# Front of an encoder block: x also loaded transposed, the norm's root applied to the results, LRU tiles read scaled between two scans

## The chip, the cores and the metric

One core of one Trainium2 chip. The metric is the device time of one execution in microseconds; 1294.04 us is the median of three runs (1293.98 to 1294.94). TensorE (PE) multiplies into eight PSUM banks of 128 x 512 float32. VectorE (DVE), ScalarE (ACT) and GpSimd (POOL) do elementwise work; SyncE (SP) only issues transfers here. Each engine runs its own list of instructions in order and waits on semaphores.

## The reference, cut to what matters

The kernel computes one encoder block: 16 meta tokens are put ahead of 1024 tokens, a group of recurrent heads (RG-LRU) and an attention group (MLA) share one input projection, and a ConvGLU feed-forward follows. The change touches only the first stage:

```python
hn = rmsnorm(h, norm_mix_g)      # h / sqrt(mean(h*h) + eps) * g, per token
proj = hn @ w_in                 # 1024 -> 512 + 512 + 256 + 128 + 32
x_lru, g_lru, c_q, c_kv, k_pe = split(proj)
xc = dwconv(x_lru)               # 4 taps along the tokens
y_lru = rg_lru_bidir(xc) * gelu(g_lru)   # two scans, forward and backward
q = rmsnorm(c_q) @ w_uq;  kv = rmsnorm(c_kv) @ w_ukv
```

The root of the norm belongs to a token and the gain g to a column of h. So `proj` can be had either from the normalised tokens, or from the raw tokens times (g * w_in), with each token's column of the result multiplied by its 1/root afterwards. Where a second rmsnorm follows (c_q, c_kv) the token's factor cancels, but for eps.

## The kernel before, in words

All products of the front are made of three fp32r products: each float32 operand is split into a high part (a copy rounded to fp32r) and a low part (value minus high), and `split_products` (L100 to L102) issues high*high, high*low and low*high.

The normalised, transposed tokens are kept in `xn_h` and `xn_l` (128 partitions x 8 k-blocks x 1040 tokens). Before the change a tile of 128 tokens (token-major) goes through a chain over four engines: SP loads it into one of four `x_tm` buffers, ACT squares it with a running sum (L440), DVE makes the variance (L652), ACT takes the root (L445), DVE takes the reciprocal (L658) and scales the tile by root and gain (L663), PE transposes it in eight matmuls (L889), ACT copies the high part out of PSUM (L450) and DVE the low part (L669). There are nine such tiles (16 meta tokens, then eight of 128).

The input projection is cut into twelve weight tiles of 128 columns (`tiles`): x0 to x3 (LRU input), c0 to c2 (the latents), k (rope part of the key), g0 to g3 (gate). Each weight tile is loaded (`load_w`, three buffers, a load waits until PE has finished the tile three before it), its high part made by ACT (`high_w`, L428) and its low part by DVE (`low_w`, L642). A unit is one weight tile times one stretch of tokens, 24 matmuls into one PSUM bank: x0 and c0 go in four stretches of 272 or 256 tokens as the tokens arrive, alternating, with the remaining transposes between their halves; all later tiles go in three stretches of 348 or 346.

The order of PE is written out: x0 and c0 alternating, then `order`: x1, G0, x2, c1, G1, x3, c2, G2, k, g0, G3, g1, g2, g3. G0 to G3 are the gate products of the recurrence, 12 units of three matmuls. The banks go round, so a unit waits until the earlier unit in its bank has been read (`free_bank`). ACT reads x, k, g and G out of PSUM, and squares and copies c (L469, L470); DVE makes the low part of c (L685) and with it frees c's bank.

For each of the four LRU tiles f: the four-tap convolution on DVE (`conv`, L695, L697), its high part on ACT (L477), low part on DVE (L705), G products on PE, `gates` on ACT (L487), `decay` on ACT (L496 to L502, three table loads), `gate_in` (L710) and `recurrence` on DVE: for each direction two elementwise operations (L716, L718) and a scan (L720, L723), then a sum (L726). `gelu(f)` on ACT writes `gel`, `gate_out` on DVE multiplies (L731). DVE's and ACT's order is written out too: in both, conv(f+2) stands behind recurrence(f), and the high part of its result is made on ACT ahead of decay(f+1), whose end starts recurrence(f+1).

After g3 the queries, keys and values of nine token tiles are made, then attention, output projection and feed-forward; the change leaves their code as it is. GpSimd's work in the front is a polynomial on 128 x 8 values (`softplus`, L359 to L370) and later the rope tables.

## Time and profile before

| | us |
|---|---|
| median of three runs | 1294.04 |
| the profiled execution, its own time | 1295.26 |
| span of its trace | 1293.2 |
| TensorE busy in the span | 1272.9 |
| VectorE busy | 998.6 |
| ScalarE busy | 769.5 |
| GpSimd busy | 148.3 |

The trace is of one execution of its own. The span runs from the first to the last instruction; 2.06 us lie outside it. Times below are microseconds from the start of the span.

### The profile page before, as it was taken

To read this page: it belongs to the slowest core of one execution; us is meant where nothing else is said; L and a number is where in the kernel's file an instruction comes from. 1 tells how busy PE (TensorE), PEld (TensorE's weight loads), DVE (VectorE), ACT (ScalarE), POOL (GpSimd) and SP (SyncE) were. 2 spreads that over 40 slices of the span, in tenths; PEclk is the share of its full clock that TensorE was granted. 3 is DMA by queue.
4 is the path that set the end of the run, shared out by engine and by line. 5 is a ranking of instruction groups with operands and counts; after the bars stand their busy time and mean duration, and the time that the engine had idled before them with its cause. 6 is when DMAs were issued, how large, how long until landed. Compare 5 with 4: busy or idle time off the path is not lost.

```text
span 1293.2 us, 18580 instructions
## 1 busy us (share of the span) xinstructions
PE 1272.9 (98%) x6202; PEld 1022.0 (79%) x6202; DVE 998.6 (77%) x1507; ACT 769.5 (60%) x1154; POOL 148.3 (11%) x175
## 2 busy tenths in 40 slices
PE   7999999999999999999999999999999999999998
PEld 7999998866667666687678888888888888888886
DVE  6677569778888876676879887787878887887856
ACT  6487648577676875633445565646474565656470
POOL 3000036400000001322300001000010000000010
PEclk9999999999999999999999999999999999999999
DMA  6111200000000014200143746576574846575667
GB/s 222 34 54 41 74 1 1 1 2 9 9 10 9 10 48 165 91 9 23 62 136 87 175 109 159 126 169 134 146 170 94 191 97 170 110 170 133 164 140 250
DMA packets 40939, 123.02 MB, mean 95 GB/s; under 512 B 7378, under 2 KB 8082, under 8 KB 34484
## 3 DMA queue, kind: packets, MB, share of 16 engines
q0 software_dynamic: 7200, 52.43, 21.4%
q1 hardware_dynamic: 33684, 69.86, 15.5%
q8 instruction: 34, 0.56, 0.2%
q14 instruction: 21, 0.17, 0.0%
HBM read 62.34 MB, written 59.80 MB: 94 GB/s over the span
## 4 chain that ended last, share of the span: by engine, by line
PE 85%; DVE 7%; ACT 4%; issue 2%; DMA 1%; SPq 0%; POOL 0%; DVEq 0%; ACTq 0%
PE banks L2967 31%; PE banks L3039 15%; PE banks L100 7%; PE banks L102 7%; PE banks L101 7%; PE banks L1954 2%; PE banks L2060 2%; PE banks L2104 2%; PE banks L2107 2%; PE banks L2061 2%; PE banks L2105 2%; PE banks L2062 2%; ACT e_f L1567 1%; PE banks L1909 1%; PE banks L1933 1%
## 5 line engine op out<-in xcount | busy, mean ns | idle before, releaser
L2967 PE MATMUL banks<-x_hi,slot_h 128*128 128x512 f32 x616 | 242.9, 394 | 2.9 <-DVE slot_l L2653 1.4
L2967 PE MATMUL banks<-x_lo,slot_h 128*128 128x512 f32 x616 | 243.5, 395 | 0.0
L2967 PE MATMUL banks<-x_hi,slot_l 128*128 128x512 f32 x616 | 242.9, 394 | 0.0
L2435 ACT ACTIVATE slot_h<-up_raw 128x512 fp32r<-128x512 f32 x127 | 79.9, 630 | 174.5 <-PE banks L2967 170.2
L2967 PEld LDWEIGHTS banks<-x_hi,slot_h 128*128 128x128 f32 x616 | 115.6, 188 | 31.6 <-DVE slot_l L2653 2.2
L2967 PEld LDWEIGHTS banks<-x_lo,slot_h 128*128 128x128 f32 x616 | 115.6, 188 | 27.0
L2967 PEld LDWEIGHTS banks<-x_hi,slot_l 128*128 128x128 f32 x616 | 115.7, 188 | 26.9
L2513 ACT ACTIVATE staged<-banks 128x1024 f32<-128x1024 f32 x100 | 101.6, 1027 | 40.9 <-PE banks L3039 40.9
L3039 PE MATMUL banks<-dn_h,a_h 128*128 128x512 f32 x280 | 110.4, 394 | 0.0
L2418 POOL DMA_DIRECT2D down_sums<-staged x50 | 44.2, 885 | 571.0 <-ACT staged L2513 496.0
L3039 PE MATMUL banks<-dn_h,a_l 128*128 128x512 f32 x280 | 109.6, 391 | 0.0
L3039 PE MATMUL banks<-dn_l,a_h 128*128 128x512 f32 x280 | 109.5, 391 | 0.0
L1567 ACT ACTIVATE e_f<-banks 128x1024 f32<-128x1024 f32 (+1 forms) x72 | 73.6, 1023 | 53.1 <-PE banks L2062 49.5
L100 PE MATMUL banks<-xn_h,win_h 128*128 128x346 f32 (+5 forms) x304 | 96.5, 317 | 1.5 <-DVE xn_l L669 1.5
L1716 DVE TENSOR_REDUCE lam_t<-banks 128x1 f32<-128x512 f32 x128 | 86.7, 687 | 14.1 <-PE banks L1954 14.1
L102 PE MATMUL banks<-xn_h,win_l 128*128 128x346 f32 (+5 forms) x304 | 95.2, 313 | 0.0
L101 PE MATMUL banks<-xn_l,win_h 128*128 128x346 f32 (+5 forms) x304 | 95.1, 313 | 0.0
L2653 DVE TENSOR_TENSOR slot_l<-up_raw,slot_h 128x512 fp32r<-128x512 f32 x127 | 87.0, 685 | 4.9 <-ACT slot_h L2435 4.7
L1761 DVE TENSOR_TENSOR e_l<-e_f,e_h 128x512 fp32r<-128x512 f32 x128 | 86.9, 690 | 1.2 <-ACT e_h L1574 1.0
L2796 DVE SCALAR_TENSOR_TENSOR gate_conv<-gate,par,gate_conv 128x1024 f32<-128x1024 f32 x44 | 55.6, 1283 | 24.1 <-ACT gate_conv L2527 19.7
L1574 ACT ACTIVATE e_h<-banks 128x1024 fp32r<-128x1024 f32 x64 | 65.2, 1018 | 0.0
L2744 DVE TENSOR_TENSOR dn_l<-dn_raw,dn_h 128x512 fp32r<-128x512 f32 x70 | 48.0, 686 | 20.2 <-ACT dn_h L2499 20.2
(357 smaller groups left out, 2870.8 us busy)
## 6 DMA issues: line engine op xcount, KB each, us to landing
down_sums<-staged POOLq DMA_DIRECT2D x50, 1024.0 KB, 8.0
up_raw<-in_w_up SPq DMA_DIRECT2D x88, 256.0 KB, 3.7
dn_raw<-in_w_down SPq DMA_DIRECT2D x22, 512.0 KB, 6.7
win_raw<-in_w_in SPq DMA_DIRECT2D x11, 512.0 KB, 3.3
x_tm<-in_x_tm SPq DMA_DIRECT2D x8, 512.0 KB, 5.9
wo_raw<-in_w_out SPq DMA_DIRECT2D x16, 256.0 KB, 4.0
h<-in_x_tm SPq DMA_DIRECT2D x8, 512.0 KB, 5.7
down_sums<-h SPq DMA_DIRECT2D x3, 1024.0 KB, 6.6
```

What stands on the lines that cost most here:

```text
L100: nc.tensor.matmul(out, w_h, x_h, start=first, stop=False)
L101: nc.tensor.matmul(out, w_h, x_l, start=False, stop=False)
L102: return nc.tensor.matmul(out, w_l, x_h, start=False, stop=last)
L1567: nc.scalar.activation(e_f[g % 3][0:n], s_ps(g)[0:n], ACT.Exp, scale=SCALE)
L1574: ins = nc.scalar.activation(e_h[g % 3], s_ps(g), ACT.Exp, scale=SCALE)
L1716: ins = nc.vector.tensor_reduce(mx3[:, i:i + 1], side, AX.X, ALU.max)
L1761: nc.vector.tensor_tensor(e_l[(g - 1) % 2][:, cs], e_f[(g - 1) % 3][:, cs], f32(e_h[(g - 1) % 3][:, cs]), ALU.subtract).then_inc(sem["e_lo ...
L2435: nc.scalar.activation(s_h[slot], x, ACT.Copy).then_inc(sem["up_hi"], 1)
L2513: nc.scalar.activation(staged[b][:, 2 * p:2 * p + 2, :], bank(4 + 2 * p, 2).rearrange("p (i n) -> p i n", i=2), ACT.Copy).then_inc(sem["dn ...
L2653: nc.vector.tensor_tensor(s_l[slot], x, f32(s_h[slot]), ALU.subtract).then_inc(sem["up_lo"], 1)
L2967: ins = nc.tensor.matmul(o, s[slot][:, k], xs[w], start=fresh and k == 0 and n == 0, stop=k == 3 and n == 2, skip_group_check=not fresh)
L3039: ins = nc.tensor.matmul(bank(4 + i), x[:, ts], w, start=k in FRESH and n == 0, stop=n == 2, skip_group_check=k not in FRESH)
```

## The change

- The tokens are loaded twice: transposed and raw (`x_raw`, four stretches, the first in two halves), and token-major in pairs of tiles (`x_tm`) for the squares alone. The transposes, the scaling of tiles and the broadcast load of the gain go.
- ACT and DVE split the raw transposed tokens into high and low parts straight from SBUF.
- The gain is multiplied into each weight tile before it is split: by GpSimd (`gain_w`), for tile 1 by DVE.
- ACT squares the nine token tiles in a row; then one variance, one root, one reciprocal for all. DVE builds eight diagonal blocks of the roots, and PE multiplies them by a matrix of ones (`rows_of_r`, units R), which gives in every partition the row of all tokens' 1/root; ACT copies it to SBUF (`x_rb`).
- DVE reads the x and g tiles out of PSUM, multiplied by that row (`read_scaled`); x2 and x3 are read between the two scans of a recurrence. The gelu is one activation of 1040 columns from SBUF.
- The eps of the second norms is scaled by the token's variance (`v_kv_eps`, `v_q_eps`), and the rope part of the key is scaled when it is read.
- The banks: the eight first units have one bank each, then R, then the round starts at bank 7. PE's order of tiles stays.

```diff
+    raw_at = (M_LRU, M_YL, M_YL + 2 * P * KD, M_LRU + (META + 2 * P) * KD)
+    x_raw = [place(f"x_raw{c}", at, (KD, 2 * P + (0 if c else META))) for c, at in enumerate(raw_at)]
+    x_sb = [place(f"x_tm{b}", at, (2, D)) for b, at in
+            enumerate((M_C + T, M_C + 4 * T, M_CSQ + T, raw_at[3] + 2 * P * KD))]
+    x_rb, x_dg = place("x_rstd_rows", M_KPE + T, (T,)), place("x_diag", M_KPE + 2 * T, (XT, P))
+    x_var, x_r = stat[:, 0, 0:NT], stat[:, 0, 16:16 + NT]
+    x_std, v_kv_eps, v_q_eps = stat[:, 1, 0:NT], stat[:, 0, 48:48 + NT], stat[:, 1, 48:48 + NT]
+    mix_g = par[:, COLS["mix_g"]:COLS["mix_g"] + KD]
...
-    ST_BANK = (4 + shared) % 8
+    AT = 7
+    ST_BANK = (AT + shared) % 8
     rest = [u for u in later_units[shared:] if u[0] != "st"]
-    bank_no = [n % 4 for n in range(len(first_units))] + [(4 + n) % 8 for n in range(shared)] +\
+    bank_no = list(range(len(first_units))) + [1, 3, 5] + [(AT + n) % 8 for n in range(shared)] +\
               [ST_BANK if u[0] == "st" else (ST_BANK + 1 + rest.index(u) % 7) % 8 for u in later_units[shared:]]
+    act_reads = [u for u in units if u[0] in "RGk"]
+    dve_reads = [u for u in first_units if u[0] == "c"] + [u for u in first_units if u[0] == "x"] +\
+                [u for t in (("x", 1), ("x", 2), ("c", 1), ("x", 3), ("c", 2), ("g", 0), ("st", 0), ("g", 1), ("g", 2), ("g", 3))
+                 for u in units_of(*t)]
...
-        def load_x(j):
-
-            if j == 0:
-                sp.dma_start(x_meta[0:META], dram["meta_tm"]).then_inc(sem["x_meta_in"], 16)
-                return
-            if j > 4:
-                sp.wait_ge(sem["xn"], j - 3)
-            sp.dma_start(x_sb[(j - 1) % 4], dram["x_tm"][P * j - P:P * j, :]).then_inc(sem["xt_in"][(j - 1) % 4], 16)
+        def load_raw(c):
+
+            if c >= 2:
+                sp.wait_ge(sem["xr_in"][c - 2], 16)
+            arrived = sem["xt_in"][3] if c == 1 else sem["xr_in"][c - 2]
+            sp.dma_start(x_raw[c], dram["x_raw"][c - 1]).then_inc(arrived, 16)
+
+        def load_raw_0(w):
+            sp.dma_start(x_raw[0][:, HALVES[w]], dram["x_raw0"][w]).then_inc(sem["xr_in"][w], 16)
+
+        def load_tm(b):
...
+            if b == 3:
+                sp.wait_ge(sem["xt_in"][3], 16)
+            sp.dma_start(x_sb[b], dram["x_tm"][2 * P * b:2 * P * (b + 1), :].rearrange("(t p) d -> p t d", p=P))\
+              .then_inc(sem["xt_in"][b], 16)
...
         sp.dma_start(ident, dram["ident"]).then_inc(sem["ident_in"], 16)
-        load_x(0)
-        load_x(1)
-        sp.dma_start(mix_g, dram["mix_g"].unsqueeze(0).broadcast_to([P, D])).then_inc(sem["mix_g_in"], 16)
         load_w(0)
-        load_x(2)
+        load_raw_0(0)
         load_w(1)
-        load_x(3)
-        load_x(4)
+        load_raw_0(1)
+        load_raw(1)
+        load_raw(2)
+        load_raw(3)
+        load_tm(0)
+        sp.dma_start(x_meta, dram["meta_tm"]).then_inc(sem["x_meta_in"], 16)
+        load_tm(1)
+        load_tm(2)
+        load_w(2)
+        load_tm(3)
         load_gw(0)
-        load_w(2)
-        for j in range(5, NL):
-            load_x(j)
         for name in ("gqk", "rope_c", "rope_s"):
             sp.dma_start(con[name], dram[name]).then_inc(sem["con_in"], 16)
         load_w(3)
...
+        def gain_w(n):
+            cols = ROPE if tiles[n][0] == "k" else P
+            pool.wait_ge(sem["w_in"][n % 3], 16 * (n // 3 + 1))
+            w = w_raw[n % 3][:, :, 0:cols]
+            nc.gpsimd.tensor_tensor(w, w, mix_g.unsqueeze(2).broadcast_to((P, KD, cols)), ALU.mult).then_inc(sem["w_gain"], 1)
+
+        pool.wait_ge(sem["par_in"], 16)
+        gain_w(0)
         softplus()
+        pool.wait_ge(sem["w_gain"], 2)
+        for n in range(2, len(tiles)):
+            gain_w(n)
...
-            act.wait_ge(sem["w_in"][n % 3], 16 * (n // 3 + 1))
+            act.wait_ge(sem["w_gain"], n + 1)
...
-        def high_x(j):
-            n, t0 = LOADS[j]
-            act.wait_ge(sem["x_t"], j + 1)
-            nc.scalar.activation(xn_h[:, :, t0:t0 + n], tp(j)[:, :, 0:n], ACT.Copy).then_inc(sem["x_hi"], 1)
-            wait_unit(act, ("x", f, c))
-            nc.scalar.activation(xpad[:, 2 + c0:2 + c0 + cn], ps(("x", f, c))[:, 0:cn], ACT.Copy)\
-              .then_inc(sem["read_act"], 1)
...
+                act.wait_ge(sem["xt_in"][(j - 1) // 2], 32 if (j - 1) // 2 == 3 else 16)
+            x, i = x_of(j)[0:n], x_col(j)
+            nc.scalar.activation(x, x, ACT.Square, accum_out=x_var[0:n, i:i + 1]).then_inc(sem["x_sq"], 1)
+        def std_x():
+            act.wait_ge(sem["x_var"], 2)
+            for n, ts in PARTS:
+                nc.scalar.activation(x_std[0:n, ts], x_var[0:n, ts], ACT.Sqrt).then_inc(sem["x_std"], 1)
+        def high_x(c, w):
+            c0, cn = LOAD_CH[c]
+            act.wait_ge(sem["xt_in"][3] if c else sem["xr_in"][w], 16)
+            nc.scalar.activation(xn_h[:, HALVES[w], c0:c0 + cn], x_raw[c][:, HALVES[w]], ACT.Copy).then_inc(sem["x_hi"], 1)
+
+        def copy_r():
+            for c, (c0, cn) in enumerate(((META, 4 * P), (META + 4 * P, 4 * P), (0, META))):
+                wait_unit(act, ("R", 0, c))
+                nc.scalar.activation(x_rb[:, c0:c0 + cn], ps(("R", 0, c))[:, 0:cn], ACT.Copy).then_inc(sem["read_act"], 1)
...
-            if f:
-                act.wait_ge(sem["y_lru"], f)
-            for c, (c0, cn) in enumerate(CH):
-                wait_unit(act, ("g", f, c))
-                nc.scalar.activation(gel[:, c0:c0 + cn], ps(("g", f, c))[:, 0:cn], ACT.Gelu_apprx_tanh)\
-                  .then_inc(sem["read_act"], 1)
+            wait_read(act, ("g", f, 2))
+            nc.scalar.activation(gel, gel, ACT.Gelu_apprx_tanh).then_inc(sem["gelu"], 1)
...
+        act.wait_ge(sem["lam_e"], 1)
+        nc.scalar.activation(x_std[:, 0:1], con["lam_t"][:, 1, 0:1], ACT.Sqrt)
+
+        high_x(0, 0)
+        high_w(0)
+        high_x(0, 1)
+        high_w(1)
+        high_x(1, 0)
+        high_x(1, 1)
+        read_c(0, 0)
+        square_x(1)
+        square_x(2)
         square_x(0)
-        high_x(2)
-        std_x(3)
...
+        for j in range(5, NL):
+            square_x(j)
+        std_x()
+        read_c(0, 2)
+        high_w(2)
+        high_gw(0)
+        read_c(0, 3)
+        copy_r()
         high_xc(0)
         high_w(3)
-        for c in range(3):
-            read_x(1, c)
         high_w(4)
...
+        def gain_w(n):
+            dve.wait_ge(sem["w_gain"], n)
+            dve.wait_ge(sem["w_in"][n % 3], 16 * (n // 3 + 1))
+            nc.vector.tensor_tensor(w_raw[n % 3], w_raw[n % 3], mix_g.unsqueeze(2).broadcast_to((P, KD, P)), ALU.mult)\
+              .then_inc(sem["w_gain"], 1)
...
-        def scale_x(j):
-            nc.vector.scalar_tensor_tensor(out=xn[j % 2][0:n], in0=x_of(j), scalar=x_r[0:n, j:j + 1], in1=mix_g[0:n],
-                                           op0=ALU.mult, op1=ALU.mult).then_inc(sem["xn"], 1)
...
+        def high_low_x(c):
+            c0, cn = LOAD_CH[c]
+            dve.wait_ge(sem["xr_in"][c - 2], 32)
+            for w in range(2):
+                link(nc.vector.tensor_copy(xn_h[:, HALVES[w], c0:c0 + cn], x_raw[c][:, HALVES[w]]))
+                low_part(c, w)
+
+        def low_part(c, w):
+            c0, cn = LOAD_CH[c]
+            nc.vector.tensor_tensor(xn_l[:, HALVES[w], c0:c0 + cn], x_raw[c][:, HALVES[w]],
+                                    f32(xn_h[:, HALVES[w], c0:c0 + cn]), ALU.subtract).then_inc(sem["x_lo"], 1)
+
+        def low_x(c, w):
+            dve.wait_ge(sem["x_hi"], 2 * c + w + 1)
+            low_part(c, w)
+
+        def var_x():
+            dve.wait_ge(sem["x_sq"], NL)
+            for n, ts in PARTS:
+                nc.vector.tensor_scalar(x_var[0:n, ts], x_var[0:n, ts], 1.0 / D, EPS, ALU.mult, ALU.add)\
+                  .then_inc(sem["x_var"], 1)
+        def diag_x():
+            dve.wait_ge(sem["x_std"], 2)
+            for n, ts in PARTS:
+                link(nc.vector.reciprocal(x_r[0:n, ts], x_std[0:n, ts]))
+            dve.wait_ge(sem["ident_in"], 16)
+            nc.vector.tensor_tensor(x_dg, ident.unsqueeze(1).broadcast_to((P, XT, P)),
+                                    x_r[:, 0:XT].unsqueeze(2).broadcast_to((P, XT, P)), ALU.mult).then_inc(sem["x_dg"], 1)
+            nc.vector.tensor_scalar(x_dgm, ident[0:META, 0:META], x_r[0:META, XT:NT], None, ALU.mult)\
+              .then_inc(sem["x_dg"], 1)
+            dve.wait_ge(sem["x_var"], 2)
+            for n, ts in PARTS:
+                link(nc.vector.tensor_scalar(v_kv_eps[0:n, ts], x_var[0:n, ts], EPS, None, ALU.mult))
+                link(nc.vector.tensor_scalar(v_q_eps[0:n, ts], x_var[0:n, ts], EPS * EPS, None, ALU.mult))
+
+        def read_scaled(u, out):
+
+            c0, cn = chunk(u)
+            wait_unit(dve, u)
+            nc.vector.tensor_tensor(out, ps(u)[:, 0:cn], x_rb[:, c0:c0 + cn], ALU.mult).then_inc(sem["read_dve"], 1)
+
+        def read_x(f):
+            if f == 0:
+                dve.wait_ge(sem["set_up"], 3)
+                wait_read(dve, ("R", 0, 2))
+            else:
+                dve.wait_ge(sem["conv"], f)
+            for u in units_of("x", f):
+                c0, cn = chunk(u)
+                read_scaled(u, xpad[:, 2 + c0:2 + c0 + cn])
+
+        def read_g(f):
+            if f:
+                dve.wait_ge(sem["y_lru"], f)
+            for u in units_of("g", f):
+                c0, cn = chunk(u)
+                read_scaled(u, gel[:, c0:c0 + cn])
...
+                    if f + 2 < LF:
+                        read_x(f + 2)
...
-            wait_read(dve, ("g", f, 2))
+            dve.wait_ge(sem["gelu"], f + 1)
             nc.vector.tensor_tensor(yl[:, f, :], yl[:, f, :], gel, ALU.mult).then_inc(sem["y_lru"], 1)
...
-        scale_x(1)
+        low_x(0, 0)
         low_w(0)
+        gain_w(1)
+        low_x(0, 1)
         low_w(1)
+        low_x(1, 0)
+        low_x(1, 1)
+        high_low_x(2)
+        high_low_x(3)
+        low_c(0, 0)
+        low_c(0, 1)
+        var_x()
+        diag_x()
+        low_c(0, 2)
+        low_w(2)
+        low_gw(0)
+        low_c(0, 3)
+        read_x(0)
         conv(0)
         low_xc(0)
         low_w(3)
+        read_x(1)
         conv(1)
         low_w(4)
 
...
         low_w(9)
+        read_g(0)
+        low_w(10)
         gate_out(0)
-        low_w(10)
...
+        wait_tile(dve, ("st", 0))
+            nc.vector.tensor_tensor(kpe[0:n, ts], st_ps[0:n, ts, 16:16 + ROPE],
+                                    x_r[0:n, ts].unsqueeze(2).broadcast_to((n, m, ROPE)), ALU.mult).then_inc(sem["kpe_tm"], 1)
         nc.vector.tensor_tensor(uq_l, uq_raw, f32(uq_h), ALU.subtract).then_inc(sem["uq_lo"], 1)
-        gate_out(1)
+        read_g(1)
         dve.wait_ge(sem["ukv_hi"], 1)
         nc.vector.tensor_tensor(ukv_l, ukv_raw, f32(ukv_h), ALU.subtract).then_inc(sem["ukv_lo"], 1)
+        gate_out(1)
+        read_g(2)
         gate_out(2)
+        read_g(3)
         gate_out(3)
...
-            elif bank_no[n] >= 4:
-                pe.wait_ge(sem["x_lo"], NL)
-
-        def transpose_x(j):
-            n, _ = LOADS[j]
-            if j == 0:
...
-            for k in range(KD):
-                ins = nc.tensor.transpose(tp(j)[:, k, 0:n], xn[j % 2][0:n, P * k:P * k + P], ident[0:n, 0:n])
-            ins.then_inc(sem["x_t"], 1)
...
-                if (kind, f) == ("x", 0) and k == KD // 2 and 2 * c + 3 < NL:
-                    transpose_x(2 * c + 3)
+                if (kind, f) == ("x", 0) and k % (KD // 2) == 0:
+                    pe.wait_ge(sem["x_lo"], 2 * c + 1 + k // (KD // 2))
                 ins = split_products(nc, ps(u)[0:m, 0:cn], w_h[n % 3][:, k, 0:m], w_l[n % 3][:, k, 0:m],
                                      xn_h[:, k, c0:c0 + cn], xn_l[:, k, c0:c0 + cn], k == 0, k == KD - 1)
...
+        def rows_of_r():
+
+            for c in range(3):
+                free_bank(("R", 0, c))
+                pe.wait_ge(sem["x_dg"], 2 if c == 2 else 1)
+                if c == 2:
+                    ins = nc.tensor.matmul(ps(("R", 0, c))[:, 0:META], ones[0:META], x_dgm, start=True, stop=True)
+                else:
+                    for i in range(4):
+                        ins = nc.tensor.matmul(ps(("R", 0, c))[:, P * i:P * i + P], ones, x_dg[:, 4 * c + i],
+                                               start=True, stop=True)
+                ins.then_inc(sem["unit_done"], 1)
-            if n == 0:
-                pe.wait_ge(sem["ident_in"], 16)
-            for _ in range((10, 0, 4, 5)[n]):
-                nc.tensor.matmul(bank(3)[:, 0:P], ident, ident, start=True, stop=True)
-
-        for j in range(3):
-            warm(j)
-            transpose_x(j)
-        warm(3)
+            for _ in range(n):
+                nc.tensor.matmul(bank(7)[:, 0:P], ident, ident, start=True, stop=True)
+
+        pe.wait_ge(sem["ident_in"], 16)
+        warm(24)
         for c in range(len(LOAD_CH)):
-            pe.wait_ge(sem["x_lo"], 2 * c + 3)
             project(("x", 0, c))
-            if 2 * c + 4 < NL:
-                transpose_x(2 * c + 4)
             project(("c", 0, c))
+        pe.wait_ge(sem["set_up"], 3)
+        rows_of_r()
         for kind, f in order:
             if kind == "G":
                 gate_products(f)
```

## Rows read from the trace of the kernel before

**Rows 1.** The page, part 1: busy time and share of each engine.
```profile
PE 1272.9 (98%) x6202; PEld 1022.0 (79%) x6202; DVE 998.6 (77%) x1507; ACT 769.5 (60%) x1154; POOL 148.3 (11%) x175
```

**Rows 2.** Busy time by stretch: stretch, its length, each engine's busy time, PEclk, DMA.
```profile
0.00:18.60 18.60, 12.13 (x62) 11.57 (x62) 9.09 (x19) 12.63 (x22) 10.12 (x33) 1.00 0.83 307
18.60:48.30 29.70, 29.47 (x244) 29.05 (x245) 20.09 (x29) 16.96 (x35) 0.00 (x0) 1.00 0.22 68
```

**Rows 3.** PE's waits up to 235 us: who waited for whom, total, times, longest.
```profile
PE banks L100 <- DVE xn_l L669: 1.5, 2, 1.3
```

**Rows 4.** PE in order of time: start, duration, line, operands, idle time before.
```profile
3.77 4.64 PE L942 MATMUL banks<-ident 128*128 128x128 f32 x20 [3.77 <-DMA ident<-in_ident]
...
18.62 0.39 PE L100 MATMUL banks<-xn_h,win_h 128*128 128x272 f32 x1 [1.26 <-DVE xn_l L669]
...
28.22 1.03 PE L889 MATMUL banks<-ident,xn 128*128 128x128 f32 x8
29.01 0.36 PE L100 MATMUL banks<-xn_h,win_h 128*128 128x256 f32 x1
...
47.76 0.32 PE L100 MATMUL banks<-xn_h,win_h 128*128 128x348 f32 x1
...
59.21 0.32 PE L100 MATMUL banks<-xc_h,gw_h 128*128 128x348 f32 x1
...
116.38 0.32 PE L100 MATMUL banks<-xc_h,gw_h 128*128 128x348 f32 x1
```

**Rows 5.** Transfers of the first 20 us: GB/s in forty slices of 0.5 us.
```profile
GB/s 0 0 0 70 139 185 74 188 270 377 361 311 246 279 385 393 418 459 401 410 410 418 442 410 418 410 393 418 418 442 393 393 418 393 401 238 41 0 0 0
```

**Rows 6.** The page, part 6: transfers by line, KB, median us to landing.
```profile
win_raw<-in_w_in SPq DMA_DIRECT2D x11, 512.0 KB, 3.3
```

**Rows 7.** ACT in order of time, columns as in rows 4.
```profile
6.58 1.06 ACT L440 ACTIVATE x_sq<-x_tm 128x1024 f32<-128x1024 f32 x1
7.55 0.19 ACT L440 ACTIVATION_READ_ACCUMULATOR x_sq<-x_tm 128x1 f32 x1
...
9.36 1.06 ACT L428 ACTIVATE win_h<-win_raw 128x1024 fp32r<-128x1024 f32 x1 [1.20 <-DMA win_raw<-in_w_in]
...
88.35 0.55 ACT L470 ACTIVATE c_h<-banks,par 128x346 fp32r<-128x346 f32 x1
...
95.54 1.07 ACT L477 ACTIVATE xc_h<-xc 128x1040 fp32r<-128x1040 f32 x1 [0.40 <-DVE xc L697]
...
193.63 1.28 ACT L599 ACT_TABLE_LOAD   x1
...
196.66 0.69 ACT L623 ACTIVATE k_sq<-banks,lam_t 128x512 f32<-128x512 f32 x1 [0.58 <-PE banks L102]
```

**Rows 8.** DVE by group, 18 to 231 us: shapes, count, busy us, mean ns, idle before.
```profile
L697 DVE SCALAR_TENSOR_TENSOR xc<-xpad,par,xc 128x1040 f32<-128x1040 f32 x12 | 15.6, 1302 | 0.4
L642 DVE TENSOR_TENSOR win_l<-win_raw,win_h 128x1024 fp32r<-128x1024 f32 x10 | 12.5, 1248 | 5.3 <-ACT win_h L428 5.3
L720 DVE TENSOR_TENSOR_SCAN y_lru<-lru_a,lru_x 128x1040 f32<-128x1040 f32 x4 | 9.3, 2324 | 0.1
L695 DVE TENSOR_SCALAR xc<-xpad,par 128x1040 f32<-128x1040 f32 x4 | 3.3, 817 | 2.4 <-ACT xpad L460 2.4
L685 DVE SCALAR_TENSOR_TENSOR c_l<-banks,par,c_h 128x346 fp32r<-128x346 f32 x4 | 2.1, 570 | 0.0
```

**Rows 9.** DVE in order of time around recurrence(0) and recurrence(1).
```profile
77.24 1.24 DVE L716 SCALAR_TENSOR_TENSOR lru_w<-lru_a,lru_w 128x1040 f32<-128x1040 f32 x1 [1.88 <-ACT lru_a L502]
...
105.38 1.24 DVE L716 SCALAR_TENSOR_TENSOR lru_w<-lru_a,lru_w 128x1040 f32<-128x1040 f32 x1 [1.88 <-ACT lru_a L502]
...
116.55 1.54 DVE L685 SCALAR_TENSOR_TENSOR c_l<-banks,par,c_h 128x348 fp32r<-128x348 f32 x3
```

**Rows 10.** GpSimd in order of time, 543 to 548 us.
```profile
543.85 1.29 POOL L1399 TENSOR_TENSOR y_l<-y_lru,y_h 128x512 fp32r<-128x512 f32 x1
545.10 2.18 POOL L1399 TENSOR_TENSOR y_l<-y_mla,y_h 128x512 fp32r<-128x512 f32 x1
```

**Rows 11.** DVE in order of time, the same stretch.
```profile
544.11 2.10 DVE L1652 TENSOR_TENSOR y_sum<-y_sum,y_sq 128x1024 f32<-128x1024 f32 x1 [0.73 <-ACT y_sq L1496]
```

152 lines of the change are left out of this document (35 added, 117 removed).

## The prediction, made before the changed kernel ran

> **What bounds the kernel now.** I read the page first: PE is busy 98% of the span [rows 1]. Then the table by stretch: in the first 18.6 us PE is busy 12.1, mostly with warming products, and from 18.6 to 48.3 it is busy 29.47 of 29.70, at the full granted clock of 1.00, its 2.4 GHz level [rows 2]. PE's waits for the split tokens are 1.5 us in two, up to 235 us [rows 3]. So a microsecond taken from PE's work in the front, or from its start, is worth one as long as DVE and ACT keep up. PE's own order of time gives the marks [rows 4]: first projection 18.62, x1 from 47.76, G0 from 59.21 (called T1 below), G2 from 116.38, which is T1 + 57.2. A tile of three stretches (72 products) is 59.21 - 47.76 = 11.45, a set of G (36) half of it, 5.7.
>
> **The start.** The eight first units took 47.76 - 18.62 = 29.1. In between stand six transposes of eight products (29.01 - 28.22 = 0.79, with the slow restart about 0.9 [rows 4]: 5.4) and waits of 0.5; 23.2 stay. When can they begin after the change? The transfers: in rows 5 the sum up to 9.0 us is 2.08 MB, then 0.41 MB per us. Weight tile 0 was waited for until 9.36 [rows 7], when 2.2 MB had moved and 1.8 had been asked for up to it; so a transfer lands when some 0.4 MB more than the queue up to it has moved. The new queue, from the sizes in the diff: par, ident and w0 0.67 MB, landing 6.4; first half of stretch 0, 1.2 MB, 8.0; w1 9.2; second half 10.6; stretch 1 13.1; stretches 2 and 3 15.6 and 18.5; the token tiles two by two 21, 23.6, 26.1 and, behind w2, 29.7 (10.5 MB with what follows). GpSimd's product for w0 has 1024 columns; 512 took 1.29 [rows 10], so 2.5: 6.4 to 8.9. ACT: high x (1088 columns) 8.1 to 9.2, high w0 to 10.2 (1.06 [rows 7]). DVE: low x to 10.6, low w0 to 11.8 (1.25 [rows 8]). PE begins at 11.8 and waits 0.8 for its second half, since DVE has the gain of w1 before it (low w1 ends at 15.3, just as c0 wants it). After that DVE is ahead: two subtractions for stretch 1, then four copies and four subtractions for 2 and 3 (a copy isn't in the trace; I take 0.82 of a one-input operation [rows 8], ends 0.5 and 1.3, which change nothing) end at 25.9, four microseconds before they are due. c0's last unit ends at 11.8 + 0.8 + 23.2 = 35.8: 12.0 gained so far.
>
> **What is late next: the root, and the list behind it.** A square takes 1.15 with its sum [rows 7]; the last two wait for the last token tiles, 29.7, and end at 32.3; variance, root, reciprocals and the diagonal of 1024 columns on DVE (1.25) end at 34.8. R is eight products of 128 float32 columns, 0.23 each (4.64 for 20 [rows 4]): PE from 35.8 to 37.6. But x1 wants c0's last bank, which DVE frees at the end of a list behind the diagonal: meta diagonal and four small operations (1.0), low c (0.45, scaled from 0.57 for 346 columns [rows 8]), low w2 (1.2), low gate weights (0.7), low c: 38.5. All of it hangs on the last token tiles: a microsecond later there is one later here. And w3's gain meets it: its load goes out when x0 is done, 32.9, lands 3.3 later [rows 6], at 36.3.
>
> **The port between GpSimd and VectorE.** In rows 10 and 11 DVE's sum of 1024 columns starts at 544.11 and takes 2.10 in place of 1.25, while a GpSimd product runs until 545.14; then GpSimd's next takes 2.18 in place of 1.29. Each waits for the other's whole instruction, and the one that waits gets the next turn. From w2 on GpSimd has ten gains, 2.5 us each (the k tile 0.7). w3's takes the turn between low w2 and the low gate weights: 38.5 becomes 40.9. x1 starts at 40.9: **gained here 47.8 - 40.9 = 6.9** (ends: 9.3 without a meeting, 4.5 if w4's gain gets a turn too). T1 becomes 52.3; the four scaled reads of x0 (1.7), conv(0) (0.8 + 3 x 1.3 [rows 8]) and its split end at about 50, hidden under x1.
> The Trainium skill, "SBUF — State Buffer", section "Who interferes with whom", has the same lock for a VectorE instruction with two SBUF inputs, and frees one with a single SBUF input outside the two-port modes; by that the scaled reads out of PSUM escape and the scans and multiplies don't. If the gains never met DVE the whole sum would be 4.5 better; that is rival A.
>
> **The loop.** Times from the new T1. PE's period is 57.2 / 2 = 28.6. The round over DVE and ACT was 105.38 - 77.24 = 28.1 [rows 9]. The x tiles leave ACT: it follows G0 unit by unit, ends 6.2, high xc 7.3, and from there to the recurrence 8.8 (95.54 + 1.07 to 105.38 [rows 7, 9]): recurrence(0) at T1 + 16.1, before 18.0. But between its two scans stand three reads of 346 columns (0.57 by low c [rows 8], 1.6 in all), and the round becomes 29.8. Without the port: recurrence(1) from T1 + 46.0 to 58.4 (before 46.2 to 57.0), c2's first bank read at 59.3; G2's sixth unit wants it at 57.2 + 2.4 = 59.6. Before, it was read at T1 + 57.9 [rows 9]: 1.7 us of slack shrink to 0.3. With the port: w6 is asked for when x2 is done, 17.1, and its gain comes at 20.5, during the scan; it then holds up the multiply behind the reads by 0.8. w8's comes at 49.0, in recurrence(1): 0.8 if it waits for the scan, 2.5 if it goes before, I take 1.6. The read comes at 61.7 and **PE stops 2.1** (ends 0 and 6.9, the latter with full turns of w6, w8 and w9 in the two recurrences). In the third round gates(3) start 2 us before G3's eighth unit wants their first bank; w9 and w10 use that up and I count nothing. At its end read_g (1.6 each) and gate_out of g1 and g2 are through at T1 + 133.4, before g3 (133.9 + 2.1).
>
> **The tail.** Let T be the end of g3's last unit, 193.1 by the q products that follow at once. Before: table load at 193.63, k squares at 196.66 = T + 3.5 [rows 7]. After: DVE reads the unit (0.55) and q's first products wait, since it lies in their bank; gelu of 1040 columns 1.1, load 1.28, root; k squares at T + 4.1. **0.6 lost.** Everything behind is as before.
>
> Edits at nothing: the squares in a row (ACT is busy 17.0 of 29.7 [rows 2], and loses the reads of x), the early root on one column (loads the table at 3.1, before any token has landed), softplus behind the first gain (ends by 30, wanted at 53), the eps vectors (counted above). With the cover gone each costs its own 0.2 to 1.2.
>
> **Sum.** 6.9 - 2.1 - 0.6 = 4.2 saved. Against the profiled execution's own 1295.26 (1.2 above the median of the runs) that is 1291.1; against the median 1294.04 it is 1289.8, which I predict.
>
> **Rivals.**
> A. The port costs nothing on the path: w3 lands after the gate weights are split, w6 and w8 fall into gaps. 9.3 - 0.6 = 8.7: 1285.3. For it: DVE is idle a third of the stretch to 48.3 [rows 2]. Against: both marks lie where DVE works back to back. 0.20.
> B. The doubled load of x (4.2 MB more before w3) is the bound. At 307 GB/s, the mean of the first 18.6 us [rows 2], the last token tiles land at 34.5, and root, R and x1 are each late by 4.8: 4.2 - 4.8, so 1294.6, no change, with PE idle ahead of R. For it: twice the bytes. Against: 393 to 459 GB/s in the slices after 8 us [rows 5]; that mean is low by its ramp. 0.15. The skill's "SBUF — State Buffer", section "A bandwidth-pool intuition that's wrong (but worth ruling out)", gives HBM to one core about 358 GB/s; by that they would land 2.6 late and 1.6 be saved, 1292.4. The rows contradict it here.
> C. Slower: the port decides. If w3's and w4's gains both go before low c, x1 starts at 43.3 (4.5 gained); if w6, w8 and w9 each take a full 2.5 inside a recurrence, the read of c2 comes at T1 + 66.5 and PE stops 6.9: 4.5 - 6.9 - 0.6 = -3.0: 1297.0. It decides from 6.3 us of PE stops behind x1's start. For it: the one that waits gets the next turn [rows 10, 11]. Against: each gain must meet a busy stretch at its beginning. 0.12.
> D. The forecast: 0.53, its own range 1287.5 to 1292.
>
> **Range and chances.** 1285.2 to 1295.5 takes in A's price, B and the half of C next to it; the ends of the unknown costs (9.3 to 4.5 at x1, 0 to 6.9 in the loop) are reached only when they fall together. Faster by over 0.2% (2.6 us, about what a measurement of this kernel tells from no change): A, and D but for its upper end, 0.70. Within: B and that end, 0.18. Slower: C, 0.12.
>
> **What would show it.** First projection at 11.8 (after 14: the gain of w0 or the transfers). x1 at 40.9, PE idle before it, and DVE's low gate weights lasting about 3 us beside GpSimd's gain. The diagonal before R's turn; a wait of PE for it is B. A wait of PE inside G2 for low c, with lengthened multiplies beside gains. k squares 0.6 later behind g3 than before. I am wrong if G2 has no wait, or if PE's time from x1 to the k squares grows by over 5 us.

## The result: 0.19% slower, and the profile after

The changed kernel takes 1295.95 us (median of 20 runs, 1291.13 to 1301.74), the one before 1293.47 (20 runs on the same chip, 1291.81 to 1297.27). The ratio is 1.0019, 95% interval 1.0010 to 1.0028: 2.5 us slower where 4.2 less had been forecast. The time goes with the granted clock of TensorE, averaged over each run: the run at 0.999 took 1291.13, ten at 0.996 or 0.997 took 1293.1 to 1296.4, the one at 0.992 took 1301.74. The profiled execution has 1295.51 of its own (span 1293.3, mean clock 0.996).

The page, part 1, the same view as [rows 1]: PE is busy 3.1 us less in a span of the same length, POOL 26.6 us more.

```profile
PE 1269.8 (98%) x6158; PEld 1019.5 (79%) x6158; DVE 1010.2 (78%) x1521; ACT 760.5 (59%) x1123; POOL 174.9 (14%) x186
```

PE in order of time, the same view as [rows 4]. The row that stands by itself is of the kernel before: the start of its k tile, which [rows 4] lack.

```profile
3.68 8.38 PE L994 MATMUL banks<-ident 128*128 128x128 f32 x48 [3.68 <-DMA ident<-in_ident]
11.81 0.37 PE L100 MATMUL banks<-xn_h,win_h 128*128 128x272 f32 x1
...
34.94 1.95 PE L988 MATMUL banks<-x_diag,ones 128*128 128x128 f32 x16
...
39.76 0.40 PE L100 MATMUL banks<-xn_h,win_h 128*128 128x348 f32 x1 [2.55 <-DVE c_l L737]
...
52.81 0.32 PE L100 MATMUL banks<-xc_h,gw_h 128*128 128x348 f32 x1
...
109.99 0.32 PE L100 MATMUL banks<-xc_h,gw_h 128*128 128x348 f32 x1
...
116.39 0.65 PE L100 MATMUL banks<-xc_h,gw_h 128*128 128x346 f32 x1 [3.87 <-DVE c_l L737]
...
122.39 0.32 PE L100 MATMUL banks<-xn_h,win_h 128*32 128x348 f32 x1
...
193.11 0.32 PE L102 MATMUL banks<-xn_h,win_l 128*128 128x346 f32 x1
194.24 0.41 PE L100 MATMUL banks<-uq_h,c_h 128*128 128x384 f32 x1 [0.81 <-DVE gelu L705]
```

```profile
122.07 0.32 PE L100 MATMUL banks<-xn_h,win_h 128*32 128x348 f32 x1
```

x1 begins 8.0 us earlier than before (39.76 against 47.76). Two stops of PE stand before a bank that DVE has to free, 2.55 before x1 and 3.87 inside G2. From x1 to G0 it is 13.05 in place of 11.45, from G0 to G2 57.18 in place of 57.17, and from G2 to the k tile 12.40, which took 5.69 before (116.38 to 122.07). The same stretches in the table of windows, the view of [rows 2]; the last column but two is the granted clock.

```profile
36.00:40.00 4.00, 1.45 (x12) 1.26 (x12) 4.00 (x5) 1.27 (x3) 2.90 (x2) 1.00 0.44 131
40.00:44.00 4.00, 4.00 (x17) 4.00 (x17) 3.89 (x6) 0.00 (x0) 0.98 (x1) 0.57 0.00 0
44.00:60.00 16.00, 16.00 (x103) 16.00 (x102) 11.86 (x13) 9.42 (x16) 0.00 (x0) 1.00 0.04 4
112.00:116.00 4.00, 0.52 (x4) 0.24 (x2) 3.97 (x4) 2.23 (x6) 1.91 (x1) 0.91 0.22 83
116.00:122.00 6.00, 5.61 (x19) 5.61 (x20) 5.89 (x8) 2.76 (x6) 0.00 (x0) 0.50 0.01 3
122.00:150.00 28.00, 28.00 (x182) 24.23 (x182) 20.24 (x17) 16.36 (x19) 2.19 (x1) 1.00 0.11 34
```

This is the reading that the prediction lacks: behind each stop the clock is at its lower level (1.2 GHz, 0.50 in the row) for some microseconds, while PE is busy all the time. In the second row the level changed inside the stretch, hence 0.57. A product of 346 columns then takes 0.29 from start to start and not 0.16. The 5.61 that PE is busy from 116 to 122 hold 19 matmuls; at 0.16 each it would be 35.

An estimate from the mean clocks: 0.996 over a span of 1293 us is 10.3 us at the lower level (0.004 x 1293.3 / 0.5), which is what the two places hold, summed from rows of 1 us that are not shown (3.4 and 6.8). Fourteen of the 20 runs stand at 0.996 or below, so the traced execution is no exception; at 0.992 it would be 20.7.

Why the stops are there is seen in DVE and GpSimd in order of time (DVE's rows are the view of [rows 9]; its first row belongs to the start, below).

```profile
9.43 1.22 DVE L652 TENSOR_TENSOR win_l<-win_raw,win_h 128x1024 fp32r<-128x1024 f32 x1
...
35.74 2.88 DVE L652 TENSOR_TENSOR win_l<-win_raw,win_h 128x1024 fp32r<-128x1024 f32 x1
38.54 0.68 DVE L663 TENSOR_TENSOR gw_l<-gw_raw,gw_h 128x512 fp32r<-128x512 f32 x1
39.14 0.47 DVE L737 SCALAR_TENSOR_TENSOR c_l<-banks,par,c_h 128x256 fp32r<-128x256 f32 x1
39.54 1.42 DVE L705 TENSOR_TENSOR xpad<-banks,x_rstd_rows 128x272 f32<-128x272 f32 x4
...
100.03 1.24 DVE L768 SCALAR_TENSOR_TENSOR lru_w<-lru_a,lru_w 128x1040 f32<-128x1040 f32 x1 [1.88 <-ACT lru_a L532]
...
102.58 3.91 DVE L772 TENSOR_TENSOR_SCAN y_lru<-lru_a,lru_x 128x1040 f32<-128x1040 f32 x1
106.41 1.34 DVE L705 TENSOR_TENSOR xpad<-banks,x_rstd_rows 128x348 f32<-128x348 f32 x3
...
113.72 2.12 DVE L652 TENSOR_TENSOR win_l<-win_raw,win_h 128x256 fp32r<-128x256 f32 x1
115.77 1.53 DVE L737 SCALAR_TENSOR_TENSOR c_l<-banks,par,c_h 128x348 fp32r<-128x348 f32 x3
```

```profile
35.64 1.90 POOL L404 TENSOR_TENSOR win_raw<-win_raw,par 128x1024 f32<-128x1024 f32 x1 [6.08 <-DMA win_raw<-in_w_in]
38.64 2.35 POOL L404 TENSOR_TENSOR win_raw<-win_raw,par 128x1024 f32<-128x1024 f32 x1 [1.10 <-DMA win_raw<-in_w_in]
...
102.00 2.31 POOL L404 TENSOR_TENSOR win_raw<-win_raw,par 128x1024 f32<-128x1024 f32 x1 [16.41 <-DMA win_raw<-in_w_in]
113.65 1.91 POOL L404 TENSOR_TENSOR win_raw<-win_raw,par 128x1024 f32<-128x1024 f32 x1 [9.35 <-DMA win_raw<-in_w_in]
```

Three instructions of DVE last as long as their own work and what is left of GpSimd's gain: low w2 2.88 in place of 1.22, the scan 3.91 in place of 2.33, low w of the k tile 2.12 in place of 0.42. Each ends about its own duration behind the gain's end (37.54, 104.31, 115.56). The durations alone are those of other runs: 1.22 in no_gain_pool, 2.33 there and in [rows 8], 0.42 in short_reads.

The Trainium skill, "SBUF — State Buffer", section "Who interferes with whom", says that a VectorE instruction with two SBUF inputs is shut out for the whole GpSimd instruction if that one has begun; here the scan, which the prediction's rows did not show beside GpSimd, follows it too. The four scaled reads of x0 take one operand out of PSUM; they ran beside w4's gain (38.64 to 40.99) and took 1.42, as they do with no GpSimd product near (1.43 in no_gain_pool). So that gain, which rival C feared, cost nothing.

The tail on ACT, the view of the last of [rows 7].

```profile
194.02 1.07 ACT L536 ACTIVATE gelu<-gelu 128x1040 f32<-128x1040 f32 x1 [5.93 <-DVE gelu L705]
195.11 1.28 ACT L609 ACT_TABLE_LOAD   x1
...
198.01 0.69 ACT L633 ACTIVATE k_sq<-banks,lam_t 128x512 f32<-128x512 f32 x1 [0.58 <-PE banks L102]
```

The k squares stand at 198.01 where they stood at 196.66. What is behind them, to the end of the span, took 1093.9 to 1097.5 us in the profiled executions of all thirteen kernels here, without regard to the change. So for the front their place tells more than a single time, and I give it for each kernel. (It was 1095.3 in after's profiled execution and 1096.5 in before's; that is why the 1.35 doesn't show in their own times.) But the place holds the start's own scatter: the first projection came at 18.62 in before's trace and at 17.42 in that of before_stop, whose start is the same, and between 10.40 and 12.26 in the eleven kernels with the new start. A difference of places under some 2 us is not to be read without it.

### The profile page after: what moved, and what is told of

Same layout as the page of the kernel before. It is cut to its first block, busy times and chain, and to the rows that moved or that the text cites. A ratio compares the mean times of both kernels' runs of the same rounds, so it can differ in the third digit from the quotient of the medians.

```text
span 1293.3 us, 18476 instructions
## 1 busy us (share of the span) xinstructions
PE 1269.8 (98%) x6158; PEld 1019.5 (79%) x6158; DVE 1010.2 (78%) x1521; ACT 760.5 (59%) x1123; POOL 174.9 (14%) x186
## 4 chain that ended last, share of the span: by engine, by line
PE 83%; DVE 7%; ACT 4%; DMA 3%; issue 2%; SPq 0%; POOL 0%; DVEq 0%; ACTq 0%
PE banks L3016 31%; PE banks L3088 15%; PE banks L100 7%; PE banks L101 6%; PE banks L102 6%; PE banks L2003 2%; PE banks L2109 2%; PE banks L2153 2%; PE banks L2110 2%; PE banks L2111 2%; PE banks L2156 2%; PE banks L2154 2%; DMA x_tm<-in_x_tm 1%; ACT e_f L1616 1%; PE banks L1958 1%
```

## The experiments

All times are medians beside runs of the kernel before on the same chip, 15 to 29 of them, whose medians are 1293.79, 1293.24 and 1293.76 in the three groups. "Under before" goes by these.

### Fill the stops

```diff
+                    for _ in range(12):
+                        nc.tensor.matmul(ps(("R", 0, c))[:, 384:512], ident, ident, start=True, stop=True)
...
+                if f == 2 and (d, w, c) == (0, 1, 1):
+                    for _ in range(17):
+                        nc.tensor.matmul(ps(u)[:, 384:512], ident, ident, start=True, stop=True)
```

> The changed kernel with 29 idle products added: twelve of 128 float32 columns before the last product of the roots' row, seventeen before the fifth gate unit of the third LRU tile, just where PE stands still for 2.55 and 3.87 us in the changed kernel's trace. They do no useful work. Theory (the stops cost twice: themselves, and a granted clock of 0.50 for some 3 us of the products behind the first and 6 us behind the second): with PE busy through both places the clock stays at 1.00, the marks x1 and k keep the stops' length but lose 1.6 and 2.6 us of slow products, 4.2 us less than the changed kernel: about 1291.5, 0.15% under the kernel before. Rival (the slow products have nothing to do with the stops, and come at the same places or others anyway): the same as the changed kernel, 1295.5 to 1296. Rival (the spread of the changed kernel from run to run is elsewhere, in attention or the feed-forward): the spread of 1291 to 1302 stays.

Measured: 1291.18 (1290.07 to 1292.59, 11 runs), ratio 0.9978 (0.9969 to 0.9987), 2.6 under before; after has 1.0019, so 0.41% better than that. The clock was 0.999 or 1.0 in all eleven. k squares at 194.50, though the first projection was 0.45 later than in after. DVE is as late as in after (the scan takes 3.91 again); only the clock is different:

```profile
36.00:44.00 8.00, 8.00 (x62) 7.85 (x61) 6.66 (x9) 1.73 (x4) 4.35 (x2) 1.00 0.21 66
...
116.00:122.00 6.00, 6.00 (x40) 4.97 (x39) 5.89 (x6) 4.31 (x8) 0.00 (x0) 1.00 0.14 44
```

What follows: the work that the change adds isn't what makes it slower. Without the lower clock it is faster than before with the stops left as they are; the idle products do nothing but keep PE occupied. It isn't the 4.2 of the forecast either: the stops are still there.

### The same stop in the kernel before

```diff
             dve.wait_ge(sem["c_hi"], c_units.index(("c", k, c)) + 1)
+            if (k, c) == (2, 0):
+                for _ in range(9):
+                    link(nc.vector.scalar_tensor_tensor(out=c_l[:, k, c0:c0 + cn], ...))   # the same low part again
```

> The kernel before, with nine repeats of low c(2,0) on DVE (0.6 each, 5.4 in all) in front of the real one; the slack there is 1.7, so PE stops in G2 for about 3.7. If a stop of that length by itself lowers the granted clock, as I read the trace of after, G2 then runs for some microseconds at 0.50 and costs 2.5 more: 1300. Rival: the lower clock came from something else in the changed kernel; then only the stop is paid: 1297.5, at a granted clock of 1.00 behind it.

Measured: 1299.27 (1297.56 to 1303.13, 4 runs), ratio 1.0052 (1.0033 to 1.0071), 6.0 over before; k squares at 201.09, and 5.6 later than before when both are taken from their first projection. PE's stop, and the windows behind it:

```profile
121.51 0.42 PE L100 MATMUL banks<-xc_h,gw_h 128*128 128x346 f32 x1 [3.80 <-DVE c_l L689]
```

```profile
123.00:126.00 3.00, 3.00 (x13) 3.00 (x12) 2.89 (x4) 2.05 (x5) 0.00 (x0) 0.50 0.00 0
```

What follows: a stop of 3.80 is enough, in a kernel that has neither the gains nor the scaled reads. From G2 to the k tile 11.31 passed (115.18 to 126.49) in place of 5.69: 3.80 for the stop and 1.8 for the clock. The lower level came 1.5 us behind the restart and held for 3.3; in after it was there before the restart (0.65 on average from 115 to 116) and held for 5.7 behind it. The stop is the same to 0.1, its price isn't: 1.8 in one execution, 2.8 in the other. Two of the kernels below keep this stop in G2 as it is, and their traces give two prices more: 3.1 in w2_split_early (12.62 from G2 to the k tile) and 1.6 in tail_split (11.16).

```profile
112.35 0.66 PE L100 MATMUL banks<-xc_h,gw_h 128*128 128x346 f32 x1 [3.88 <-DVE c_l L740]
```

```profile
116.11 0.66 PE L100 MATMUL banks<-xc_h,gw_h 128*128 128x346 f32 x1 [3.89 <-DVE c_l L743]
```

### Leave out the gains on GpSimd

```diff
-        for n in range(2, len(tiles)):
-            gain_w(n)
```

The weights of tiles 2 to 11 are used without their gain; ACT's `high_w` waits for their transfer instead.

> The changed kernel without GpSimd's gain products for weight tiles 2 to 11 (the norm's gain is left out of these tiles; tiles 0 and 1 keep it). Theory (GpSimd's products take the port from VectorE at three places of the path): low w2 takes 1.2 in place of 2.9 and x1 starts at about 38.0 instead of 39.8; the scan of recurrence(1) takes 2.3 instead of 3.9 and low w7 0.4 instead of 2.1, so the stop in G2 shrinks from 3.9 to under 0.6; with the clock that no longer falls in G2, 7 to 8 us less than the changed kernel: 1288 to 1289. Rival (the three reads between the scans alone make the loop late, the port doesn't matter): the stop in G2 stays above 2 us and the time above 1293. Rival (a wait of TensorE for something else takes its place, for instance the gate of the last tile): less than 4 us less.

Measured: 1285.56 (1284.72 to 1291.51, 6 runs), ratio 0.9941 (0.9922 to 0.9960), 8.2 under before; k squares at 187.93, 10.1 before those of after. This is more than I had expected (1288 to 1289), since both stops go, and with them the clock: x1 begins at 37.73 behind a wait of 0.87, PE has no wait in G2, and low w2 and the scan have their own durations.

```profile
35.38 1.22 DVE L652 TENSOR_TENSOR win_l<-win_raw,win_h 128x1024 fp32r<-128x1024 f32 x1
```

### Reorder what DVE does around each stop

Low c2 into recurrence(1), low w7 behind it:

```diff
                     if f + 2 < LF:
                         read_x(f + 2)
+                    if f == 1:
+                        low_c(2, 0)
+                        low_c(2, 1)
...
+            if f == 1:
+                low_c(2, 2)
...
         recurrence(1)
         low_w(7)
-        for c in range(3):
-            low_c(2, c)
```

> The changed kernel with VectorE's list altered around recurrence(1): the low parts of c2 (which free the banks that G2 waits for) stand behind the reads of x3 between the scans (stretches 0 and 1) and before the last sum (stretch 2), and low w7 comes behind them. Same work, same gains on GpSimd. Theory (the stop of 3.9 us in G2 is VectorE's order: the banks are freed last in its list): the stop becomes 0 to 0.8, the clock stays up in G2, 5.5 to 6.5 us less than the changed kernel: 1289.5 to 1290.5. Rival (VectorE's total load is the bound, so the stop only moves to a later unit or to conv(3)): under 3 us less, a stop of PE in G3 or g0 in its place.

Measured: 1291.80 (1288.62 to 1294.74, 12 runs), ratio 0.9981 (0.9971 to 0.9991), k squares at 192.08. That is 1.3 over the range I had expected, which was for a clock of 1.00 in G2 and the stop before x1 as in after. The stop in G2 is 0.56. The twelve runs scatter with the clock, though not by it alone: 1288.62, 1289.02 and 1291.80 at 1.0, 1292.62 and 1294.74 at 0.997. In the profiled one the stop before x1 had no price:

```profile
39.42 0.40 PE L100 MATMUL banks<-xn_h,win_h 128*128 128x348 f32 x1 [2.39 <-DVE c_l L737]
```

```profile
40.00:44.00 4.00, 4.00 (x27) 4.00 (x27) 3.89 (x5) 0.00 (x0) 0.64 (x1) 1.00 0.00 0
```

Low w2 ahead of the variance (with its high part ahead of ACT's last two squares), and both low c straight behind the diagonal:

```diff
         for j in range(5, NL):
+            if j == 7:
+                high_w(2)
             square_x(j)
...
-        high_w(2)
...
         low_c(0, 1)
+        low_w(2)
         var_x()
         diag_x()
         low_c(0, 2)
-        low_w(2)
-        low_gw(0)
         low_c(0, 3)
         read_x(0)
+        low_gw(0)
         conv(0)
+        eps_x()
```

> The changed kernel with the lists altered before x1 alone: ScalarE's high w2 between the squares, VectorE's low w2 ahead of the variance, low c(0,2) and low c(0,3) straight behind the diagonal, the low gate weights and the eps vectors after the scaled reads of x0. Theory (the stop of 2.55 us before x1 is a list of VectorE, lengthened by the gain of w3 on GpSimd): x1 starts at 36.9 to 37.3 in place of 39.8, the clock stays at 1.00 there, 4.0 us less than the changed kernel: about 1292. Rival (the roots' row is the bound: squares of the last token tiles): x1 not before 38.5, under 1.5 us less. In both the stop in G2 stays.

Measured: 1292.20 (1289.33 to 1292.97, 11 runs), ratio 0.9984 (0.9975 to 0.9992), k squares at 194.19. As expected, PE has no wait before x1, and the one in G2 stays:

```profile
37.21 0.43 PE L100 MATMUL banks<-xn_h,win_h 128*128 128x348 f32 x1
```

```profile
PE banks L100 <- DVE c_l L740: 3.9, 1, 3.9
```

Both together:

> Both reorderings together: w2's split and low c(0,2), c(0,3) ahead of the gate weights, and low c2's first banks inside recurrence(1). My theory (two meetings of GpSimd's gain with VectorE, each turned into a PE stop that also lowers the clock): x1 at about 37.2 with no stop, 10.5 under before; in G2 only small waits, up to 1.7 together; the tail keeps its 1.1; the clock stays at 1.00. k squares at 188.5 to 190, the time 1285.5 to 1287, 7 to 8 under before. Rival (a loss taken away in one place comes back at the next, since DVE is full): the two savings overlap, k squares at 192 or later and 1290 or more.

Measured: 1287.92 (1286.46 to 1290.42, 6 runs), ratio 0.9954 (0.9939 to 0.9969), 5.3 under before; k squares at 190.07. Against after, by the differences of their ratios to before, one edit saves 0.38% (4.9 us), the other 0.35% (4.5), both 0.65% (8.4). So the two stops are two costs that nearly add. The clock was 0.999 or 1.0 in all six. It came out 0.9 over the range that I had given; small waits remain (0.6 in G2, 0.3 ahead of the k tile, 0.3 in G3).

### Take the scaled reads out of the round

```diff
-                read_scaled(u, xpad[:, 2 + c0:2 + c0 + cn])
+                read_scaled(u, xpad[:, 2 + c0:2 + c0 + cn]) if f < 2 else read_two(u, xpad[:, 2 + c0:4 + c0])
```

> Left out: the scaled reads of x2 and x3 take 2 columns each instead of 346 to 348 (the rest of the buffer keeps x1), so the 1.34 that stand between the two scans in after fall to about 0.2. If the longer round is a part of the stop in G2, as the prediction's 1.6 had it, the stop falls from 3.87 to 2.7 (the two lengthened DVE instructions remain), and the slow clock behind it is rarer: 1293 to 1294.5 against 1296 for after. Rival: only the meetings with GpSimd count, the reads lie in a wait for the exponentials, the stop stays at 3.9 and the time at 1296.

Measured: 1290.90 (1288.23 to 1293.09, 11 runs), ratio 0.9974 (0.9964 to 0.9984), k squares at 192.25: 2.1 us better than my best case. DVE in order of time, then PE in G2:

```profile
102.13 3.91 DVE L777 TENSOR_TENSOR_SCAN y_lru<-lru_a,lru_x 128x1040 f32<-128x1040 f32 x1
105.96 0.26 DVE L710 TENSOR_TENSOR xpad<-banks,x_rstd_rows 128x2 f32<-128x2 f32 x3
...
112.20 0.42 DVE L652 TENSOR_TENSOR win_l<-win_raw,win_h 128x256 fp32r<-128x256 f32 x1
```

```profile
113.17 0.43 PE L100 MATMUL banks<-xc_h,gw_h 128*128 128x346 f32 x1 [1.11 <-DVE c_l L742]
```

The three reads cost 1.08 less. But the list came 1.5 earlier to low w7 and was past it before w9's gain began (113.18): the meeting was missed, another 1.7. A stop of 1.11 is left, behind which the clock stays at 1.00. So one microsecond on DVE was worth nearly three of PE's stop, and some more of clock.

### Two other ways to have the gain

Scaled copies on ACT and scaled subtractions on DVE, eight of 128 columns per tile, and no GpSimd:

```diff
+                for k in range(KD):
+                    ins = nc.scalar.activation(w_h[n % 3][:, k, 0:cols], w_raw[n % 3][:, k, 0:cols], ACT.Copy,
+                                               scale=mix_g[:, k:k + 1])
```

> The product is complete here: for tiles 2 to 11 GpSimd's gain is replaced by scaled copies on ACT (eight of 128 columns per tile) and scaled subtractions on DVE (eight per tile). No GpSimd work meets DVE in the front. If the meetings are what costs: x1 at about 38, scan of recurrence(1) back at 2.33, stop in G2 under 1, clock 1.00, 1286 to 1287.5 (the kernel without any gain for these tiles had 1285.6; ACT has some 1.0 and DVE 0.5 more work per tile). Rival: ACT and DVE pay more for eight short instructions than the meetings cost, the recurrences come later, G2 stops by 2 or more, and the time is 1290 or over.

Measured: 1290.71 (1287.09 to 1292.90, 12 runs), ratio 0.9976 (0.9966 to 0.9987), k squares at 191.01. The rival was nearer: its time came, its stop of 2 or more in G2 did not. Eight short instructions cost DVE 2.19 for low w2, less than the 2.88 of the meeting and more than its 1.22; PE waits 2.2 before x1 and 1.6 in G2, and the clock is 1.00 behind both.

```profile
35.55 2.19 DVE L658 SCALAR_TENSOR_TENSOR win_l<-win_raw,par,win_h 128x128 fp32r<-128x128 f32 x8
```

Four gains of 256 columns on GpSimd in place of one of 1024:

```diff
+            for h in ([slice(0, KD)] if n == 0 else [slice(k, k + 2) for k in range(0, KD, 2)]):
+                w = w_raw[n % 3][:, h, 0:cols]
+                ins = nc.gpsimd.tensor_tensor(w, w, mix_g[:, h].unsqueeze(2).broadcast_to((P, w.shape[1], cols)), ALU.mult)
```

> The changed kernel with GpSimd's gains of tiles 2 to 11 cut into four instructions of 256 columns (about 0.5 each). If an instruction of DVE waits for one whole GpSimd instruction, the scan of recurrence(1) takes at most 2.9 in place of 3.9 and low w7 at most 1.8; but each following DVE instruction can meet one more quarter. Theory: the four quarters alternate with DVE's instructions, the total lost is between one and four quarters; G2's stop is 2 to 3 in place of 3.87, the clock falls less, 1292 to 1294. Rival: the total is the same 1.9 per gain whatever its pieces, or more, since four instructions of GpSimd cost more than one: stop of 3.9 or more, 1296.

Measured: 1290.44 (1286.09 to 1291.31, 6 runs), ratio 0.9967 (0.9952 to 0.9982), k squares at 191.40; better than the 1292 to 1294 expected. The turns alternate: DVE pays a part of a quarter at several instructions, GpSimd the rest.

```profile
101.25 2.62 DVE L774 TENSOR_TENSOR_SCAN y_lru<-lru_a,lru_x 128x1040 f32<-128x1040 f32 x1
```

```profile
100.71 4.71 POOL L405 TENSOR_TENSOR win_raw<-win_raw,par 128x256 f32<-128x256 f32 x4 [13.08 <-DMA win_raw<-in_w_in]
```

The scan pays 0.3 in place of 1.6, the multiply behind the reads 0.2, and GpSimd's four last 4.71, where four beside an idle DVE took 2.33; nobody waits for GpSimd there. PE stops 1.0 in G2 and the clock stays. Before x1 it stopped for 1.7, and there the clock did fall, to 0.50 from 39 to 42 us.

### The tail

```diff
+            if f == 3:
+                for c, (c0, cn) in enumerate(CH):
+                    wait_read(act, ("g", f, c))
+                    ins = nc.scalar.activation(gel[:, c0:c0 + cn], gel[:, c0:c0 + cn], ACT.Gelu_apprx_tanh)
```

> The last gelu (1040 columns, 1.07, only after DVE has read all of g3) in three pieces, each behind its own read. Theory: behind the last read only 346 columns are left, so table load and k squares come 0.6 earlier behind g3's end: 4.0 in place of 4.6; PE's wait of 0.8 for the read stays. Rival: what holds the k squares is PE's late start of the q products, not the gelu, and the distance stays at 4.6.

Measured (one profiled run, 1293.28): the rival holds. ACT's last piece takes 0.49 and not 1.07, and nothing behind it moves: from the start of g3's last product to the k squares 4.92 (191.59 to 196.51), in after 4.90.

```profile
192.50 0.49 ACT L538 ACTIVATE gelu<-gelu 128x346 f32<-128x346 f32 x1 [3.07 <-DVE gelu L711]
193.00 1.28 ACT L615 ACT_TABLE_LOAD   x1
196.51 0.69 ACT L639 ACTIVATE k_sq<-banks,lam_t 128x512 f32<-128x512 f32 x1 [0.58 <-PE banks L102]
```

In both kernels, and in the one before, ACT waits 0.58 for PE ahead of the k squares, so ACT isn't what holds them. It is PE's late start: the first q product comes 1.13 behind the start of g3's last one in after (0.81 of it is the wait for the read of the bank), where it came 0.16 behind before (192.79 and 192.95). That is the 1.0.

### All that the runs spoke for

Both reorderings, the gains in quarters and the gelu in three.

> Everything that the runs spoke for: both reorderings, GpSimd's gains in four pieces, the last gelu in three. x1 at 36.5 to 37.2, stops in G2 under 1 in all, the clock at 1.00, k squares 4.0 behind g3: k squares at 188.5, 1285.5 to 1287, some 0.5% under before (both reorderings alone had 1287.9). Rival: four GpSimd instructions per gain meet more DVE instructions than one, and where the reorderings have already put the meetings off the path this only lengthens DVE's lists: 1288 or more.

Measured: 1287.17 (1285.99 to 1289.98, 5 runs), ratio 0.9958 (0.9944 to 0.9971), 6.6 under before by the medians, 0.42% by the ratio; k squares at 189.13. The time is 0.2 over the expected range, the k squares 0.6 later. PE waits 0.8 for the diagonal, and its list of waits names no other for DVE until g3's end; the clock is 1.00 in both stretches:

```profile
36.00:60.00 24.00, 24.00 (x156) 23.85 (x155) 21.17 (x28) 14.12 (x22) 5.04 (x8) 1.00 0.14 54
100.00:150.00 50.00, 49.24 (x318) 44.73 (x316) 41.29 (x36) 30.48 (x49) 17.18 (x15) 1.00 0.13 42
```

By their ratios to before it beats both kernels. Against the two reorderings alone (0.9954) the intervals overlap: whether quarters and split gelu add anything isn't shown.

## Why the prediction was wrong, step by step

- **The start**: right in number, in part by luck. First projection forecast for 11.8, seen at 11.81; but low w0, which was to set it, was ready at 10.65 (9.43 + 1.22; the gain of w0 took 1.89 and not 2.5). PE had no wait there: its idle products at the start, 24 of them in 48 records, ran from 3.68 until then, and the prediction has no term for them. In short_reads and tail_split they were through sooner, PE waited for low w0, and began at 10.61 and 10.71. c0's end was forecast for 35.8, seen at 34.94; the diagonal came at 34.5 (34.8 forecast), ACT began the square of the last pair at 30.1 (29.7 forecast). Rival B is out: PE did not wait for the roots. R took 1.95 (1.8 forecast), again with luck: a product of 128 float32 columns makes two records (16 for R's first eight), so the 20 of [rows 4] are ten products, at 0.46 each and not 0.23.
- **x1**: 40.9 forecast, 39.76 seen, 8.0 gained and not 6.9. The meeting with w3's gain was there, at low w2 and not at the gate weights, which took 0.68 where some 3 were forecast.
- **The clock behind that stop**: not in the sum. 13.05 - 11.45 = 1.6 lost.
- **G0 to G2**: no change, as forecast. Recurrence(1) at T1 + 47.2; with w6's meeting 46.8 was forecast.
- **The stop in G2**: forecast 2.1, measured 3.87. This is a term of wrong size. I counted one meeting in recurrence(1), at 1.6, and the trace has it (3.91 - 2.33). w9's gain met low w7 as well, 1.7 (2.12 - 0.42); I had it in rival C's upper end and not in the forecast. That meeting is nearly the whole difference: the recurrence began 0.4 later than forecast (47.2 against 46.8) and took 13.7 in place of 14.0.
- **The clock behind it**: not in the sum. 12.40 - 5.69 - 3.87 = 2.8 lost.
- **The tail**: 0.6 forecast, 1.0 measured (4.90 against 3.87), and by another way: PE's wait, which the prediction named without following it to the k squares, and not gelu and table load.

In k squares: forecast 6.9 - 2.1 - 0.6 = 4.2 earlier; seen 8.0 - 1.6 - 3.9 - 2.8 - 1.0 = 1.3 later. Of the 5.5 between them 4.4 are the clock. The step that failed is therefore the prediction's sum: it priced each stop of PE at its length ("PE stops 2.1"), with the clock at 1.00 behind it. Its own sign for this came true: PE's time from x1 to the k squares grew by 9.4 (148.90 to 158.25), where over 5 was to mean that it is wrong. Two runs show it from both sides: filling the stops turns after into a kernel 0.22% faster than before, and the same stop put into before costs 6.0 by the medians for a stop of 3.8.

Rival C had the sign right and the mechanism half: GpSimd's meetings do decide. But it set its point at 6.3 us of stops, priced at their length; in after 3.9 in G2 were enough, with the clock behind it.

By the medians after is 2.5 slower, by this one execution 1.35. The difference is within what the runs of after vary (1291.1 to 1301.7); only one of them is traced, so the price of a stop in each of them is not shown.

What stays open is what decides the price. Ahead of x1, stops of 2.2 and 2.39 cost nothing in the profiled executions of two kernels, 2.41, 2.47 and 2.55 cost 1.6 in three others, and 1.66 cost as much in one (x1 to G0 13.05 to 13.07 in place of 11.45). In G2 stops of 1.0, 1.1 and 1.6 cost 0.3 beyond their length, at a clock of 1.00, and the four of 3.8 to 3.9 cost 1.6, 1.8, 2.8 and 3.1. No run varied a stop alone in small steps.

## What to carry to other kernels

In a kernel that is bound by TensorE a stop of it isn't priced at its length: ask what the clock does behind it. Here stops of 1.7 to 3.9 us cost from nothing to 3.1 more, and the median holds a part of that price (after's spread is 10.6 us, with the stops filled 2.5). Put what frees a bank first in its engine's list: two reorderings without one instruction more or less took 8.4 us off a change that had seemed a loss. And work moved to an idle engine that can shut another out, as GpSimd does VectorE here, is to be priced where its input lands, in each round, against each instruction of the other engine that can be running then; cut into pieces it costs the other less at a time.

## What the runs showed of the hardware that was not expected

- A scan of 1040 columns on DVE is held up by a running GpSimd product like an elementwise operation: 3.91 in place of 2.33.
- GpSimd's product of 1024 columns with a broadcast gain takes 1.90, less than twice the 1.29 of 512 columns [rows 10].
- What a running GpSimd product does to DVE depends on the instruction: reads of PSUM with one operand in SBUF kept their time beside it (1.42 for four), while the first operation of the convolution (128x1040, one operand, in SBUF) took 1.64 in short_reads beside the gain from 113.18 to 115.08, and 0.82 alone.
- The same stop of 3.8 to 3.9 lowered the clock before the restart in one execution and 1.5 us after it in another; its price was 1.6 to 3.1 in four.
